# Delta-rule mixers: the output gates' projection moved into the core as plain products

## The reference, cut to what matters

```python
def hybrid_mixer(h, w_in, ...):           # h = rmsnorm(x, norm1)
    proj = h @ w_in                       # 512 x 2706
    (dn_q, dn_k, dn_v, dn_z, dn_a, dn_b, fx_q, fx_k, fx_v, fx_f, pl_x) = split(proj)
    o_dn = gated_deltanet(dn_q, dn_k, dn_v, dn_z, dn_a, dn_b, ...)
    o_fx = forgetting_attention(fx_q, fx_k, fx_v, fx_f, ...)
    o_pl = pool_mixer(pl_x, pool_w, pool_scale)
    return concatenate([o_dn, o_fx, o_pl]) @ w_out

def gated_deltanet(q, k, v, z, a, b, ...):
    q, k, v = silu(causal_conv(q, k, v))  # then l2norm of q and k
    o = chunk_gated_delta_rule(q, k, v, g, beta)   # chunks of 64, states passed on
    return rmsnorm(o, onorm_g) * silu(z)
```

## Time and profile before

| | us |
|---|---|
| median of three runs | 2748.19 |
| profiled execution | 2746.75 |
| its span | 2744.9 |
| TensorE busy | 2617.0 (95%) |
| VectorE busy | 1577.5 (57%) |
| ScalarE busy | 1193.3 (43%) |
| GpSimd busy | 317.1 (12%) |

### The profile page before, as it was taken

The page is one execution under the profiler, slowest core; times in us unless marked ns, Lnnn a source line. Parts: engine busy times, 40 slices in busy tenths (PEclk is TensorE's granted clock), DMA queues, the critical chain, the costliest instruction groups (busy, mean ns, idle before and its releaser), DMA issues. The chain is left out here.

```text
span 2744.9 us, 54730 instructions
## 1 busy us (share of the span) xinstructions
PE 2617.0 (95%) x22741; PEld 2102.6 (77%) x22741; DVE 1577.5 (57%) x1951; ACT 1193.3 (43%) x1531; POOL 317.1 (12%) x360
## 2 busy tenths in 40 slices
PE   8999999999999988999999998998899999999998
PEld 7676778888777767788888887854778797788887
DVE  6747454244484655677667676466565545454462
ACT  5644343132455443556555655245224433432232
POOL 6022000000110401011111111021410000000002
PEclk9999899999999999999999999999999999999999
DMA  4200244334220022877877786302023352234341
GB/s 138 81 10 3 62 114 110 83 92 111 71 91 20 4 55 95 284 278 276 291 277 277 280 292 210 104 19 77 2 60 113 91 153 69 75 96 106 91 110 52
DMA packets 351883, 331.12 MB, mean 121 GB/s; under 512 B 17273, under 2 KB 269525, under 8 KB 351605
## 3 DMA queue, kind: packets, MB, share of 16 engines
q1 hardware_dynamic: 348101, 317.76, 37.1%
q0 software_dynamic: 3392, 11.14, 1.1%
q10 hardware_dynamic: 240, 0.07, 0.0%
HBM read 317.41 MB, written 11.53 MB: 120 GB/s over the span
## 5 line engine op out<-in xcount | busy, mean ns | idle before, releaser
L3141 DVE TENSOR_TENSOR experts_w_lo<-experts_raw,experts_w_hi 128x2048 fp32r<-128x2048 f32 (+1 forms) x81 | 167.6, 2080 | 75.4 <-ACT experts_w_hi L3097 72.0
L3141 DVE TENSOR_TENSOR experts_w_lo<-raw_in_act,experts_w_hi 128x2048 fp32r<-128x2048 f32 (+1 forms) x81 | 167.0, 2078 | 59.6 <-ACT experts_w_hi L3097 59.2
L3097 ACT ACTIVATE experts_w_hi<-raw_in_act 128x2048 fp32r<-128x2048 f32 (+1 forms) x81 | 140.0, 1750 | 50.4 <-DMA raw_in_act<-in_moe_up 44.9
L3310 PE MATMUL experts_psum<-experts_w_hi,experts_xg_lo 128*128 128x512 f32 x384 | 155.0, 404 | 5.2 <-DVE experts_w_lo L3141 4.0
L1563 PE MATMUL proj_psum<-keep_act_hi,proj_w_lo 128*128 128x512 f32 x360 | 151.0, 419 | 7.5 <-DVE proj_w_lo L1483 7.4
L3311 PE MATMUL experts_psum<-experts_w_lo,experts_xg_hi 128*128 128x512 f32 x384 | 150.7, 392 | 0.0
L3312 PE MATMUL experts_psum<-experts_w_hi,experts_xg_hi 128*128 128x512 f32 x384 | 150.4, 392 | 0.0
L3097 ACT ACTIVATE experts_w_hi<-experts_raw 128x2048 fp32r<-128x2048 f32 (+1 forms) x81 | 140.4, 1743 | 19.7 <-DMA experts_raw<-in_moe_gate 16.0
L1565 PE MATMUL proj_psum<-keep_act_hi,proj_w_hi 128*128 128x512 f32 x360 | 140.5, 390 | 0.0
L1564 PE MATMUL proj_psum<-keep_act_lo,proj_w_hi 128*128 128x512 f32 x360 | 140.3, 390 | 0.0
L831 PE MATMUL conv_ffn_psum<-keep_act_hi,conv_ffn_w_lo 128*128 128x512 f32 x336 | 131.9, 393 | 2.0 <-DVE conv_ffn_hid_lo L880 2.0
(11 more groups left out here) (893 smaller groups left out, 6791.6 us busy)
## 6 DMA issues: line engine op xcount, KB each, us to landing
raw_in_act<-in_moe_gate SPq DMA_DIRECT2D x33, 1024.0 KB, 9.1
experts_raw<-in_moe_up SPq DMA_DIRECT2D x32, 1024.0 KB, 10.3
experts_raw<-in_moe_down SPq DMA_DIRECT2D x32, 768.0 KB, 9.9
raw_in_act<-in_moe_down SPq DMA_DIRECT2D x32, 768.0 KB, 6.8
conv_ffn_raw<-in_w_ffn_in SPq DMA_DIRECT2D x43, 512.0 KB, 5.0
experts_raw<-in_moe_gate SPq DMA_DIRECT2D x17, 1024.0 KB, 8.8
raw_in_act<-in_moe_up SPq DMA_DIRECT2D x16, 1024.0 KB
proj_raw<-in_w_in SPq DMA_DIRECT2D x18, 768.0 KB, 4.3
```

The lines of the kernel that those rows point to most:

```text
L3097: act.activation(w_hi[v % 2][:, s], raw[ring][:, 0:n], ACT.Copy).then_inc(rounded, 1)
L3141: dve.tensor_tensor(w_lo[v % 2][:, s], raw[ring_of(2 * v + q)][:, 0:n], w_hi[v % 2][:, s].bitcast(F32), ALU.subtract).then_inc(split, 1)
L3310: pe.matmul(out, lhs[1][:, first + k, :], w_hi[slot][:, cols], start=begin and k == 0, stop=False)
```

## The change

- The group of `z` is taken out of the projection (seven groups, 14 halves). The pieces of `dn_aside` behind half 8 move one half earlier. The pooling products move from half 10 to half 6. The head sums of the attention's k stand together in half 12, each with a bank of its own.
- POOL copies the root of the norm, `norm.rstd`, into a tile that stays for the core.
- In the core, SP loads the three tiles of `z`'s weights into buffers that the projection has left (ahead of the tile for the next phase). POOL multiplies them by the gain of the norm. TensorE multiplies them with `m.xT` in plain float32, 8 products a tile, 24 in all: the first tile from before the last `first_level` to n = 1, the second at n = 16 to 20, the third at n = 24 to 29, behind the attention's piece. ACT copies each tile out of its bank, POOL multiplies it by the root, ACT applies Silu behind the scan, and DVE waits for that before it weighs.
- The banks of `first_level` change (6, 5, 6), `swap_halves` of the second pair waits for the second starting value, and the attention's blocks of output wait for the tile of `z` before theirs in bank 7.
- The core opens with 18 turns of the identity instead of 9, and the setup has 20 ahead of its wait for the parameters.

```diff
@@ setup_phase, tensor
+            pe.wait_ge(copied_even, 1)
+            turn_identity(m, pe, ps[:, 0, P:2 * P], 20)
             pe.wait_ge(filled, 16 * len(places))
@@ dn_aside, gpsimd
+        norm.root_ready(pool)
+        pool.wait_ge(rows_done, 13)
+        pool.tensor_copy(fab[:, 0, :], norm.rstd[:, :]).then_inc(root_kept, 1)
...
@@ dn_aside, vector
-        if h in (10, 11, 12):
+        if h in (9, 10, 11):
...
-            expand(dve, h - 10)
-        if h == 14:
+            expand(dve, h - 9)
+        if h == 12:
             head_norm(dve, 0)
             head_norm(dve, 1)
@@ dn_aside, tensor
+        if (h, f) == (6, 0):
+            pe.wait_ge(landed, 16)
+            pe.wait_ge(pooled, MEANS)
+            pooling(pe, 0)
+            pooling(pe, 1)
...
-        if (h, f) == (11, 1):
+        if (h, f) == (10, 1):
             pe.wait_ge(made, 2)
             spread_out(pe, 0, 2, 3)
...
@@ dn_core_phase
+        Z_BANK = (7, 7, 4)
+        for p, steps in enumerate(((-3, -3, -2, -2, -1, -1, 0, 1), (16, 17, 18, 18, 19, 19, 20, 20), (24, 24, 25, 26, 26, 27, 28, 29))):
...
+            def weigh(p):
+                pool.wait_ge(z_landed[p], 16 * len(r.z_weights[p]))
...
+                    pool.tensor_tensor(tile, tile, gain[:, n * kt:(n + 1) * kt].unsqueeze(2).to_broadcast([P, kt, P]), ALU.mult).then_inc(z_ready, 1)
...
+            pool.wait_ge(own_2, 2)
+            weigh(0)
             for p in range(pairs):
                 pool.wait_ge(formed, 2 * p + 1)
...
-            turn_identity(m, pe, ps[:, 7, 0:P], 9)
+            turn_identity(m, pe, ps[:, 7, 0:P], 18)
+            def gate_tile(n):
...
+                    last = pe.matmul(ps[:, Z_BANK[p], :], r.z_weights[p][k // kt][:, k % kt, :], m.xT[:, k, :], start=k == 0, stop=k == DT - 1)
...
                 attention.tensor(pe, SCAN + 2 * c)
+                gate_tile(SCAN + 2 * c)
                 pe.wait_ge(u_new, c + 1)
...
@@ mixer
-                                                              (1932, fxp[:, 3:6]), (1152, dn[:, 9:12]), (2316, fxp[:, 6:9]))]
+                                                              (1932, fxp[:, 3:6]), (2316, fxp[:, 6:9]))]
```

More of the change, by code:

```diff
@@ L1707, in scalar @@
             taps_of(act, 1)
+            for n, (j, o, _) in enumerate(groups):
+                act.wait_ge(p_full, n + 1)
+                act.activation(xp[o:o + HD, j, :], ps[o:o + HD, pool_bank(j, o // HD), :], ACT.Copy,
+                               scale=col(m, f"pool_scale_{l}", j)[o:o + HD]).then_inc(p_kept, 1)
         if h == 6:
@@ L1746, in scalar @@
                 act.activation(fsq_k[:, t, :], fxp[:, 3 + t, :], ACT.Square).then_inc(fsquared, 1)
-        if h == 13:
+        if h == 12:
             keep(act, 3, r.a_tok, 1)
             head_log(act, 0, 2)
+            for t in range(3):
+                head_log(act, 1, t)
             keep(act, 4, r.bd_tok, 1)
-            head_log(act, 1, 0)
+            act.wait_ge(flogged, 6)
+            act.activation(fsq_q, fsq_q, ACT.Exp, scale=-0.5).then_inc(frooted, 1)
             keep(act, 5, r.a_tok, 2)
-            head_log(act, 1, 1)
+            act.activation(fsq_k, fsq_k, ACT.Exp, scale=-0.5).then_inc(frooted, 1)
             keep(act, 6, r.bd_tok, 2)
-            head_log(act, 1, 2)
-        if h == 14:
[L1757 to L1762, removed]
+        if h == 13:
             act.wait_ge(fnormed, 3)
@@ L1968, in tensor @@
             head_sum(pe, 0, 2)
-        if h == 14:
+            for t in range(3):
+                head_sum(pe, 1, t)
+        if h == 13:
             pe.wait_ge(kept, 3 + f)
             turn(pe, (kd, az, kd)[f], (1, 2, 2)[f])
-            head_sum(pe, 1, f)
-        if h == 16:
+        if h == 14:
             for p in range(3):
@@ L2224, in _ @@
                 attention.gpsimd(pool, n)
+                if n in (9, 11):
+                    pool.wait_ge(masked, pairs + n + 1)
+                    weigh((n - 7) // 2)
             for n in range(LEVELS, attention.STEPS):
                 attention.gpsimd(pool, n)
+            for p in range(pairs):
+                scale(p)
         @block.tensor
@@ L2400, in _ @@
         def _(sp):
+            for p in range(pairs):
+                kt = DT // len(r.z_weights[p])
+                for n, tile in enumerate(r.z_weights[p]):
+                    sp.dma_start(tile, r.z_source[p][:, n * kt:(n + 1) * kt, :]).then_inc(z_landed[p], 16)
             m.early.load(sp, then)
@@ L2428, in _ @@
                 attention.scalar(act, n)
+                if n in (20, 30):
+                    keep_gate(n // 10 - 1)
+            act.wait_ge(z_scaled, 2)
+            act.activation(r.z_t[:, 0:2, :], r.z_t[:, 0:2, :], ACT.Silu).then_inc(z_gated, 2)
             for t, tile in reversed(list(enumerate(ready))):
@@ L2432, in _ @@
                 act.activation(m.act_hi[:, pairs + t, :], tile, ACT.Copy).then_inc(rounded, 1)
+            act.wait_ge(z_scaled, 3)
+            act.activation(r.z_t[:, 2, :], r.z_t[:, 2, :], ACT.Silu).then_inc(z_gated, 1)
             for p in range(pairs):
@@ L2460, in first_level @@
                 dve.wait_ge(p1_full, p + 1)
-                dve.tensor_tensor(x[:, p], eight(m.eye[:, :]), one(6 + p % 2), ALU.add).then_inc(x_new, 1)
+                dve.tensor_tensor(x[:, p], eight(m.eye[:, :]), one(FIRST_BANK[p]), ALU.add).then_inc(x_new, 1)
             differences(0)
@@ L2596, in mixer @@
             r.w_t, r.r_t, r.y_t, r.z_t = dn[:, 0:3], qd, dn[:, 3:6], dn[:, 9:12]
+            by_k = lambda tiles: tiles.rearrange("p a t -> p (a t)").rearrange("p (k n) -> p k n", n=P)
+            r.rstd = fab[:, 0]
+            r.z_weights = [[by_k(dn[:, 0:2])], [by_k(dn[:, 3:5])], [by_k(dn[:, 5:6]), by_k(fab[:, 3:4])]]
+            r.z_source = [k_major(w)[:, :, 1152 + p * P:1152 + (p + 1) * P] for p in range(3)]
             ready = [fxp[:, 6 + t, :] for t in range(3)] + [xp[:, t, :] for t in range(2)]
```

111 lines of the change are left out of this document (75 added, 36 removed).

## The result

| | median, us | range of runs | profiled span |
|---|---|---|---|
| before | 2748.88 | 2746.09 to 2751.27 | 2744.9 |
| changed | 2759.82 | 2753.32 to 2776.59 | 2756.2 |

The ratio is 1.0047 (95% interval 1.0031 to 1.0063): the change costs 11 us, where I had forecast no change (2747.6, range 2734 to 2758). A second series gave 1.0044 (1.0030 to 1.0057).

The account below looks back on a forecast made before the run. TensorE bounds the projection; the core is a ring of DVE and TensorE steps with some TensorE idle. Terms summed to -0.6 us: 2746.2 against 2746.75 profiled, 2747.6 as median; no-change range 2742.7 to 2753.7, overall 2734 to 2758.

Parts of the forecast that it names:

- The projection's saving, 2 x -15.5: Projection with fewer halves: 15.5 us saved a layer, 12.5 or 19.8 if chains differ.
- Half 10, 14.9 us: Projection's half 10: the old half 11 (10.6 us) plus a new 4.3 us TensorE wait for DVE's expand.
- They go to half 6 ... so nothing there.: Pooling products moved to half 6 cost nothing, as half 7 behind it waited 2.06 us for DVE anyway.
- The end 3.7 us behind TensorE: Projection's tail on ACT and DVE ends 3.7 us after TensorE, against 2.9 before.
- The opening, 2 x 6.1: Core's opening, with the products of steps 0 and 1: 6.1 us longer a layer, bounds 1.7 to 8.5.
- The scan, 2 x 11.1: Core's scan, products placed ahead of S or U: 11.1 of 13.8 us paid a layer, bounds 7.6 and 13.8.
- the port, 1: POOL's added two-input work slows DVE through shared SBUF interfaces: +1 us for both layers.
- The clock, -6: Denser TensorE work in scans and readings brings back full clock: 6 us saved, bounds 0 and 10.
- Setup, -0.5: Twenty identity turns fill 3.15 us idle in the setup, before the projection's clock fall: -0.5 us, bounds -1.2 and 0.
- The projection keeps its time: Rival: l2_of and head-norm chains each come 2 us later, 4 us a layer; 2755 us, chance 0.09.
- The ring takes them all: Rival: scan's U and S pay all 13.8 us, clock back by only 3; 2756 us, chance 0.15.
- The idle time takes the products: Rival: scan costs 8 instead of 11, clock returns all 10, no projection fall; 2736 us, chance 0.35.

Follow-up runs that it names:

- e1: Changed kernel plus 40 useless identity transpositions on TensorE in the wait of half 10 of each projection; 2812.70 us.
- e5: Changed kernel plus four plain 128x512 products in half 10's wait, and 44 instead of 52 filler turns ahead of the experts' loop; 2750.41 us, ratio 1.0006.
- e0: The changed kernel measured once more, unedited, beside the kernel before; 2759.82 us, ratio 1.0044.
- e2: Changed kernel with ACT's four pooled copies moved to the head of its half 7; 2750.46 us, ratio 1.0018.
- e6_cross: Kernel before with 26 instead of 52 filler turns ahead of the experts' loop; 2818.82 us, ratio 1.0248.
- e6_stay: Kernel before with 30 instead of 52 filler turns ahead of the experts' loop; 2837.95 us, ratio 1.0321.
- e4: Changed kernel with six of eight products of each gate tile left out, 18 of 24 a layer; 2787.55 us.
- e8: Changed kernel without 18 of 24 gate products a layer, plus 36 identity turns in half 10's wait, restoring the experts' loop's place; 2733.81 us.
- e7: Changed kernel with both e5's edits and e2's moved copies; 2744.75 us, ratio 0.9989.

## Why the prediction was wrong

The step that failed is the projection's saving. The cores came out within 2 us of the forecast in sum, with their stages mis-sized in opposite directions.

- **The projection's saving, 2 x -15.5.** Measured -8.9 and -9.9, so 12.2 us less than forecast, or 10.7 with the 1.5 that I had set apart for the clock there. The spans missed the forecast by 11.9 us in all: these 10.7, 2.1 in the cores, and 0.9 the other way in what is left. (1) *Half 10, 14.9 us.* The wait was 4.34 us, right to the tenth, but its second price was the fall of the clock: 2.7 to 3.1 us a layer where I had put 1.5 for both layers. I had the sign and argued from one fall in two openings; filled (e1, e5), half 10 takes 15.4. (2) *"They go to half 6 ... so nothing there."* Half 7 was indeed no longer. I followed the pooling products and not the four copies that ACT makes of them: 2.8 us in the queue ahead of the rounding of weights, 1.8 us in half 9, and more where the clock falls behind it (e0). The pooling products themselves cost 0.4 in half 6. With the copies moved, half 9 is back at 13.4 (e2). (3) *The end 3.7 us behind TensorE.* It was 4.5 (164.0 to 168.5).
- **The opening, 2 x 6.1, and the levels.** This term held 1.7 us for steps 0 and 1, and the scan's held 0.7 for step 16, so I had forecast 4.4 us for the opening and 2.4 for the levels. They took 5.3 and 6.1, and 3.9 and 5.6: the four products of a layer's levels (3.4 us) were paid whole. Part of the second opening is the clock, granted at 0.87 there and at 1.00 before. POOL weighs 128x1024 in 1.90 us, not 2.5.
- **The scan, 2 x 11.1, and the port, 1.** The steps listed add up to 11.2, of which 10.5 lie from step 18 on. Measured 4.2 and 7.4, with the clock back in it. The two old scans differ by 4.8 us for 12.8 us more of half clock, 0.37 us for each; by that the old scan would take some 29 us at full clock (an estimate), and the new one takes 38.3 at 1.00. So the products cost about 9 us there: the ring takes them, somewhat less than I had put. TensorE's idle time in a core fell only from 14.2 to 10.9 and from 15.5 to 12.1 us.
- **The clock, -6.** The first core had 23.9 us of half clock and now has 10.2, so at most 6.9 us come back. The second has 10.2 before and after, but 6.8 of it now lie in the opening, where there was none. From profile to profile this varies. The old cores also run in e6_cross and e6_stay: from DVE's clearing to TensorE's last reading the two take 241.4, 242.0 and 242.2 us together. The new ones take 266.8 to 273.0 in nine profiles, the changed kernel's being the longest. So the cores cost 25 to 32 us, and the forecast's terms for them sum to 29.4.
- **Setup, -0.5.** The first half starts 0.9 us earlier.
- **The rivals.** "The projection keeps its time" (0.09) named the right place: 2755 (its own sum is 2755.6) for 2759.8, by other late arrivals than it named. "The ring takes them all" comes as near in time, with 2756, but by a place that the runs bear out only in part: the scan took some 9 of 12 us. "The idle time takes the products" is refuted by e4 and e8: 18 products out, 11 us or more a layer back at an equal clock.
- **What I took for signs.** The core's start was to be near 163 us and was 168.5: this sign alone would have told. The idle of 4 us came, and so did the scans, 39.9 and 38.3 for 38 to 41. Opening and levels were to take 84 to 85 us and took 87.8 and 90.0.

Why range and chances failed: I bounded the projection's chains by 3 us but priced the clock behind a stall as an estimate without its upper end, and the change had no margin on TensorE to set against it: 24 products cost 20.6 us there for 16.0 saved.

Not tried: a spread into a free bank with the turns behind it reordered, so that TensorE would not wait at all; and doing the first gate tile's own products in that wait instead of idle ones.

## What to carry to other kernels

When an operation is moved, follow it on every engine that reads its result, not on the one that was full: the copies on ACT cost 1.8 us a layer in a half where TensorE had nothing new. A stall in dense work can be paid a second time by the clock behind it: here 4.3 us idle cost another 2.7 to 3.1, and useless products in the wait took that away. And before a total is believed, compare the fetches of instructions: 44 to 160 instructions more or fewer ahead of a long loop moved the whole by some 50 to 90 us here.

## What the runs showed of the hardware

- **A loop's place in the program.** A loop of 1,721 TensorE instructions runs without fetches behind its first pass when it starts at 16,423, 16,433, 16,439 or 16,679, and fetches about 8 blocks of 16,384 bytes a pass at 16,279, 16,381, 16,389 and 16,583. The price is 47 to 73 us over 8 passes. The kernel before stands at least 10 and fewer than 44 instructions above the border.
- **Idle time and clock.** In the dense products of the projection, over both layers of all profiles with the changed core: behind 4.34 us idle the clock was at half for 6.8 us in seven cases of eight and for 3.4 in the eighth; behind 2.6 us idle for 3.4 us in both cases; behind 1.93 to 1.99 us idle (half 9) for 3.4 us in 5 of 14 cases and not at all in 9; behind 0.9 us in none of six. The same code does not always get the same clock.
- **A later stretch at half clock.** Two runs of one kernel (e7), of 2759.0 and 2745.2 us, are told apart by one stretch behind the experts, seen here at a granted clock of 0.50 and of 0.96, with fewer instructions done in the same time. From the experts' last product to the end they take 1088 and 1074 us:

```profile
2011.40:2055.80 44.40, 41.90 (x588) 0.50 0.16 43
```

```profile
2011.40:2055.80 44.40, 40.61 (x639) 0.96 0.28 76
```

  Nothing in the code differs, and what starts it stays open. It is 14 us, as much as the whole effect of the change, so spans of profiles of which one holds it and one lacks it must not be compared as they are. The profiles before and after both lack it.
